# Weight sums made in the mixing stage and kept in DRAM for FFN 2 of a macaron decoder layer

## The reference

```python
def swiglu(h, w_gate, w_up, w_down):
    return (jax.nn.silu(h @ w_gate) * (h @ w_up)) @ w_down
...
x = x + 0.5 * swiglu(rmsnorm(x, ffn1_norm), ffn1_w_gate, ffn1_w_up, ffn1_w_down)
h = rmsnorm(x, mix_norm); proj = h @ w_in          # 40 blocks of weights: the mixing stage
...                                                # latent attention, HGRN2 recurrence, w_out, cross attention
x = x + 0.5 * swiglu(rmsnorm(x, ffn2_norm), ffn2_w_gate, ffn2_w_up, ffn2_w_down)
```

## Time and profile before

| | |
|---|---|
| median of 3 runs | 1886.82 us |
| the profiled execution | 1885.84 us, of which its instructions span 1884.0 us |
| TensorE: matmuls, share of the span, granted clock | 8824, 100%, 1.0 of full speed (the 2.4 GHz level) in all slices |
| TensorE's weight loads, VectorE, ScalarE, GpSimd: share of the span | 84%, 84%, 58%, 5% |
| DMA | 362.57 MB, 192 GB/s over the span, 57.4% of the 16 engines' time |
| chain of waits, by engine | TensorE 87%, VectorE 9%, issue 2%, ScalarE 1%, GpSimd 1% |

### The profile page before, as it was taken

How to read it: one execution, slowest core, us unless ns; L and a number is a source line. 1 busy time by engine, 2 the same in 40 slices (tenths; PEclk the granted TensorE clock), 3 DMA queues, 4 the chain that set the end, 5 groups by cost and what they waited for, 6 DMA issues and landing times.

```text
span 1884.0 us, 23266 instructions
## 1 busy us (share of the span) xinstructions
PE 1877.4 (100%) x8824; PEld 1575.1 (84%) x8824; DVE 1573.7 (84%) x2015; ACT 1087.4 (58%) x1473; POOL 95.4 (5%) x98
## 2 busy tenths in 40 slices
PE   9999999999999999999999999999999999999999
PEld 8888888888889888988888888888888888888987
DVE  6999999989999867755676774789999999999986
...
GB/s 337 224 196 201 193 198 193 225 201 201 181 187 213 217 224 157 167 179 179 136 156 111 206 192 139 156 181 200 201 184 195 203 205 216 204 195 184 197 192 171
DMA packets 176608, 362.57 MB, mean 192 GB/s; under 512 B 8432, under 2 KB 19696, under 8 KB 175856
## 3 DMA queue, kind: packets, MB, share of 16 engines
q1 hardware_dynamic: 176064, 360.89, 57.4%
...
...
HBM read 358.95 MB, written 2.10 MB: 192 GB/s over the span
## 4 chain that ended last, share of the span: by engine, by line
PE 87%; DVE 9%; issue 2%; ACT 1%; POOL 1%; DMA 0%; SPq 0%; DVEq 0%; ACTq 0%; POOLq 0%
PE acc L1943 16%; PE acc L1945 16%; PE acc L1944 16%; PE acc L1932 9%; PE acc L1934 8%; PE acc L1933 8%; DVE w_lo L1301 4%; PE small L1945 2%; PE small L1943 2%; PE small L1944 2%; PE small L2144 2%; PE tr L1894 1%; PE tr L1945 1%; PE tr L1943 1%; PE tr L1944 1%
## 5 line engine op out<-in xcount | busy, mean ns | idle before, releaser
L1301 DVE TENSOR_TENSOR w_lo<-w_raw,w_hi 128x1024 fp32r<-128x1024 f32 (+3 forms) x752 | 733.4, 1030 | 52.5 <-ACT w_hi L730 40.5
L730 ACT ACTIVATE w_hi<-w_raw 128x1024 fp32r<-128x1024 f32 (+4 forms) x568 | 507.9, 928 | 149.0 <-PE acc L1945 101.8
L1943 PE MATMUL acc<-w_hi,hT_hi 128*128 128x512 f32 (+1 forms) x920 | 355.0, 386 | 0.0
L1945 PE MATMUL acc<-w_lo,hT_hi 128*128 128x512 f32 (+1 forms) x920 | 353.4, 384 | 0.0
L1944 PE MATMUL acc<-w_hi,hT_lo 128*128 128x512 f32 (+1 forms) x920 | 353.1, 384 | 0.0
L1230 DVE TENSOR_TENSOR w_lo<-w_raw,w_hi 128x1024 fp32r<-128x1024 f32 (+1 forms) x184 | 218.3, 1226 | 59.6 <-ACT w_hi L730 58.2
L835 ACT ACTIVATE w_hi<-w_raw 128x1024 fp32r<-128x1024 f32 (+1 forms) x184 | 190.3, 1044 | 118.1 <-DVE w_raw L1289 72.6
L1943 PE MATMUL acc<-w_hi,actT_hi 128*128 128x512 f32 x528 | 207.1, 392 | 0.3
L1945 PE MATMUL acc<-w_lo,actT_hi 128*128 128x512 f32 x528 | 205.7, 390 | 0.0
L1944 PE MATMUL acc<-w_hi,actT_lo 128*128 128x512 f32 x528 | 205.6, 389 | 0.0
L828 ACT ACTIVATE w_hi<-w_raw 128x512 fp32r<-128x512 f32 (+3 forms) x184 | 149.4, 830 | 90.9 <-PE acc L1945 89.9
...
## 6 DMA issues: line engine op xcount, KB each, us to landing
...
w_raw<-in_ffn_w_down SPq DMA_DIRECT2D x40, 1024.0 KB, 5.3
w_raw<-in_w_in SPq DMA_DIRECT2D x36, 1024.0 KB, 5.1
...
w_raw<-in_ffn_w_up SPq DMA_DIRECT2D x26, 1024.0 KB, 5.8
```

The lines of the kernel that those rows point to most:

```text
L730: nc.scalar.activation(piece(w_hi, c % SPLIT, k0, k1, width), piece(raw, c % RAW, k0, k1, width), ACT.Copy).then_inc(hi_done, 1)
L1301: v.tensor_tensor(piece(w_lo, c % RAW, k0, k1, width), piece(raw, c % RAW, k0, k1, width), piece(w_hi, c % SPLIT, k0, k1, width).bitcast(F ...
L1943: mm(dst, lhs_hi, wh, start=first, stop=False)
L1945: return mm(dst, lhs_hi, wl, start=False, stop=last)
```

## The change

- `READY` names five up duos of FFN 2: (0,2), (0,3), (0,5), (1,0) and (1,4), the last with 384 columns. Each gets a fourth unit: its order becomes "upupuup", with plain pieces of 2, 3 and 3 k-tiles. To have a fourth set of activation sums, `H_SUMS` becomes 4 in FFN 2.
- The space for that comes from the down blocks of the first half in FFN 2: `A_SUMS` there becomes 4, their order "upupupup" with four plain pieces of 4 k-tiles. They had five units.
- Seven of the 20 units in these five duos are *ready*: units 0 and 2 of (0,2) and (0,3), unit 0 of the three others. Their weight sums are made in the mixing stage by VectorE in place (`job_first`, `job_second`, four subtractions of 128x512, in the last job 128x384), in four places of SBUF that are free at that time, from weights that SP fetches there; SP then stores them to `kept_sums` in DRAM. The seven jobs run in the steps 2, 5, 8, 20, 24, 28 and 32 of the mixing stage. SP fetches a job's weights ahead of the load of slot step + 3 and stores its sums ahead of the load of slot step + 6.
- A ready unit fetches three raw tiles and the four kept sums and has no `combine`. The other 13 units of the five duos are combined as before.

The tables and the shape of the duos:

```diff
+        H_SUMS, A_SUMS = {1: 3, 2: 4}, {1: (5, 3), 2: (4, 3)}
+        READY = {(0, 2): (0, 2), (0, 3): (0, 2), (0, 5): (0,), (1, 0): (0,), (1, 4): (0,)}
+        JOBS = [(h, b, n) for (h, b), ns in READY.items() for n in ns]
+        JOB_STEPS, JOB_PLACES = [2, 5, 8, 20, 24, 28, 32], list("ACVGGGA")
+        kept = nc.dram_tensor("kept_sums", [len(JOBS), P, 4 * NW], F32, kind="Internal").ap()
...
-                    DUOS.append(Duo(f, True, h, b, min(4, tiles - 4 * b) * P, "upupup", [0, 2, 4], [(6, 4), (10, 3), (13, 3)]))
+                    ready = READY.get((h, b), ()) if f == 2 else ()
+                    DUOS.append(Duo(f, True, h, b, min(4, tiles - 4 * b) * P,
+                                    *(("upupuup", [0, 2, 4, 6], [(8, 2), (10, 3), (13, 3)], ready) if ready else
+                                      ("upupup", [0, 2, 4], [(6, 4), (10, 3), (13, 3)]))))
                 for j in range(DB // 2):
-                    DUOS.append(Duo(f, False, h, j, NW, *(("upupupupup", [0, 2, 4, 6, 8], [(10, 3), (13, 3), (16, 3), (19, 3), (22, 2)]),
-                                                          ("upupupp", [0, 2, 4], [(6, 4), (10, 3), (13, 3), (16, 3)]))[h]))
+                    DUOS.append(Duo(f, False, h, j, NW, *(("upupupupup", [0, 2, 4, 6, 8], [(10, 3), (13, 3), (16, 3), (19, 3), (22, 2)])
+                                                          if (f, h) == (1, 0) else
+                                                          ("upupupup", [0, 2, 4, 6], [(8, 4), (12, 4), (16, 4), (20, 4)])
+                                                          if h == 0 else
+                                                          ("upupupp", [0, 2, 4], [(6, 4), (10, 3), (13, 3), (16, 3)]))))
```

SyncE, the fetch of a ready unit and the jobs' transfers:

```diff
+                    def load_ready(c, k, n):
...
+                        sp.wait_ge(slot_used, 2 * (c - RAW + 1))
...
+                        sp.dma_start(tiles[:, :, 0, 0:d.width], rows_of(wg, k, 2, cols)).then_inc(loaded[c % RAW], 16)
+                        sp.dma_start(tiles[:, 1, 1, 0:d.width], wu[(k + 1) * P:(k + 2) * P, cols]).then_inc(loaded[c % RAW], 16)
+                        sp.wait_ge(slot_used, 2 * (c + 1 - RAW + 1))
...
+                        sp.dma_start(made, kept[j].rearrange("p (k n) -> p k n", k=4)[:, :, 0:d.width]).then_inc(loaded[(c + 1) % RAW], 16)
...
+            def job_weights(j):
...
+                if earlier:
+                    sp.wait_ge(job_kept[place], 16 * earlier)
+                if place == "G" and not earlier:
+                    sp.wait_ge(ev("angles"), 1)
...
+                for u, name in enumerate(("gate", "up")):
+                    rows = rows_of(a[f"ffn2_w_{name}"][0], 2 * n, 2, slice(c0, c0 + w))
+                    sp.dma_start(tiles[:, :, u, 0:w], rows).then_inc(job_in[place], 16)
+
+            def job_store(j):
...
+                sp.wait_ge(job_made, j + 1)
...
+                sp.dma_start(dst, src).then_inc(job_kept[place], 16)
+
+            def jobs_around(m):
+
+                for j, step in enumerate(JOB_STEPS):
+                    if m == step + 6:
+                        job_store(j)
+                for j, step in enumerate(JOB_STEPS):
+                    if m == step + 3:
+                        job_weights(j)
...
                 for s in range(4):
+                    jobs_around(4 * b + s)
                     load(M + 4 * b + s, 0, rows_of(a["w_in"][0], 4 * s, 4, slice(starts[n], starts[n] + MIX_WIDTH[n])), 4, MIX_WIDTH[n])
```

VectorE, a ready unit in a duo, and the jobs in the mixing stage:

```diff
                         if kind == "u" and n:
-                            combine(d.raws[n], u0 + n, w)
-                            lo_parts(d.raws[n], RAW_PARTS, w, u0 + n)
+                            if n in d.ready:
+                                lo_parts(d.raws[n], RAW_PARTS, w)
+                            else:
+                                combine(d.raws[n], unit_number(m, n), w)
+                                lo_parts(d.raws[n], RAW_PARTS, w, unit_number(m, n))
...
-                        combine(e.raws[0], u0 + u1, e.width)
+                        if 0 not in e.ready:
+                            combine(e.raws[0], unit_number(m + 1, 0), e.width)
...
+            def job_first(j):
+
+                b = job_tiles(j)
+                dve.wait_ge(job_in[JOB_PLACES[j]], 32 * (JOB_PLACES[:j].count(JOB_PLACES[j]) + 1))
+                done(v.tensor_tensor(b[:, 0, :], b[:, 1, :], b[:, 0, :], ALU.subtract))
+                done(v.tensor_tensor(b[:, 1, :], b[:, 3, :], b[:, 1, :], ALU.subtract))
+
+            def job_second(j):
+
+                b = job_tiles(j)
+                done.wait()
+                done(v.tensor_tensor(b[:, 3, :], b[:, 3, :], b[:, 0, :], ALU.subtract))
+                done.wait()
+                v.tensor_tensor(b[:, 2, :], b[:, 2, :], b[:, 3, :], ALU.subtract).then_inc(job_made, 1)
...
             for m in range(40):
                 lo(M + m, 0, 4, MIX_WIDTH[MIX[m // 4]])
+                if m in JOB_STEPS:
+                    job_first(JOB_STEPS.index(m))
                 mixer(m)
+                if m in JOB_STEPS:
+                    job_second(JOB_STEPS.index(m))
```

More of the change, by code:

```diff
@@ L94 @@
     plains: list
+    ready: tuple = ()
     raws: list = field(default_factory=list)
@@ L249, in layer @@
         k_sq = at("k_sq", A0 + 67.5, [P, TT, ROPE])
+        job = {place: at("job_" + place, A0 + kb, [P, 4 * NW]) for place, kb in (("A", 66.5), ("C", 56), ("V", 36), ("G", 44))}
         o_mla = at("o_mla", A0 + 56, [P, TT, AH * P])
@@ L301, in layer @@
         out_done = sem("out_done")
+        job_in, job_kept = ({place: sem(f"job_{name}_{place}") for place in job} for name in ("in", "kept"))
+        job_made = sem("job_made")
         named = {}
@@ L411, in layer @@
                 fetches[r], fetches[r + 1] = 2 if duo.up else 1, 0
+            for n in duo.ready:
+                fetches[duo.raws[n] + 1] = 1
         M = slots["mix"]
@@ L428, in unit_number, with job_of @@
         def unit_number(m, n):
-            return sum(len(d.raws) for d in DUOS[:m]) + n
+            return sum(len(d.raws) - len(d.ready) for d in DUOS[:m]) + sum(i not in DUOS[m].ready for i in range(n))
+        def job_of(d, n):
+            return JOBS.index((d.half, d.block, n))
         def sums_before(f):
-            return (f - 1) * (H_SUMS + sum(A_SUMS))
+            return (f - 1) * (H_SUMS[1] + sum(A_SUMS[1]))
         def sums_number(m, n):
-            return sums_before(DUOS[m].f) + H_SUMS + sum(A_SUMS[:DUOS[m].half]) + n
+            f = DUOS[m].f
+            return sums_before(f) + H_SUMS[f] + sum(A_SUMS[f][:DUOS[m].half]) + n
         def turns_in(d):
@@ L520, in load_duos @@
                     for kind, n in d.steps():
+                        if kind == "u" and n in d.ready:
+                            load_ready(d.raws[n], d.units[n], n)
+                            continue
                         if kind == "u":
@@ L604, in _ @@
                     load(slots[2, "up", 0] + 4 * b + s, 0, rows_of(a[f"ffn2_w_{n}"][0], 4 * s, 4, slice(0, NW)), 4, NW)
+            for place in sorted(job):
+                sp.wait_ge(job_kept[place], 16 * JOB_PLACES.count(place))
             load_duos(2)
```

97 lines of the change are left out of this document (63 added, 34 removed).

## The result

The changed kernel takes **1892.76 us** (median of 7 runs, 1892.37 to 1894.46), beside 1886.79 us for the kernel before: a ratio of 1.0034, 95% interval 1.0025 to 1.0044. It is slower by 6.0 us, more than the 0.2% that a measurement can tell. I had forecast 1888.5 us and "within 0.2%". The profiled execution has a span of 1890.9 us, 6.9 more than before.

What follows compares the result with a forecast made beforehand. It took TensorE as the bound, with VectorE's splits barely ahead of it in FFN 2's up duos; -3.24 + 0.12 + 4.8 = +1.7 us gave 1887.5 profiled, 1888.5 us as median; range 1884.2 to 1893.0.

Steps and rivals of the forecast that it cites:

- within 0.2%: Whole kernel: its time would not be distinguishable from the kernel before, within 0.2% (3.8 us); chance 0.72.
- I carry no debt over: Duos behind those with late splits: VectorE regains its lead, so no loss was counted there.
- (0,2) and (0,3): "nothing": Up duos (0,2) and (0,3): unit 3's second split has a lead of 0.8 us, so no loss; 41.76 us each.
- The stalls inside (0,5), (1,0) and (1,4): Late VectorE splits in these up duos cost 1.9, 0.3 and 2.6 us, together +4.8 us.
- Rival 1: Adjacent units in up duos: VectorE is about 1.2 us further ahead, avoiding most stalls; 1884.5 us, chance 0.18.
- rival 3: Up duos: ScalarE's splits are late too after a late combine, doubling the 4.8 us loss; 1893.3 us, chance 0.12.
- the forecast's own spread: Whole kernel: the main forecast, given chance 0.55, spans 1886.5 to 1890.5 us.
- the range over all cases: Whole kernel: forecast and rivals together span 1884.2 to 1893.0 us.
- The down duos: FFN 2's first-half down duos: six more matmuls, but 1.24 us of waiting goes; together 126.10 us, +0.12 us.
- The mixing stage: Seven jobs add 18 us of VectorE work, covered by 100 us of its idle time: 0, with +3 as bound.
- The tight place: Mixing stage, job 0: its subtractions delay slot 3's splits but stay covered, with 0.5 us to spare.
- The 0.11 us surcharge of a wait: TensorE at a late split: it loses the lateness plus 0.11 us, as the next matmul comes late.

Runs made afterwards that it cites:

- Run 2: The change with (1,4)'s kept sums used for unit 0 of (0,4) instead, (0,4) and (1,4) keeping three units: 1887.91 us.
- run 5: The change with ScalarE making w_hi of the last second-side piece before its two Silus in FFN 2, no work added or removed: 1888.46 us.
- runs 6 and 7: The change with unit 2 ready instead of unit 0 in (0,5) and (1,4): 1890.38 us; the same plus ScalarE's Silus behind w_hi in FFN 2: 1884.45 us.
- under 8: Several versions; meant here: the kernel before with ScalarE's Silus behind w_hi of the last second-side piece, in both FFNs: 1885.19 us.

## Why the prediction was wrong

- **The step that failed** is the sentence "Behind the late blocks one combine less (before a duo whose unit 0 is ready) or slack in the down blocks takes VectorE back to its lead, so I carry no debt over". Only (0,2) has a ready unit 0 behind it. Behind (0,3), (0,5), (1,0) and (1,4) the next unit 0 is combined, and the second side had lost two tiles, 2.72 us of cover. Only behind (0,5) was there the slack that I counted on. Measured: 3.9 us in (0,4), (1,1), (1,2) and the down duo, where I put nothing; in (0,4) and the down duo at unit 0, in (1,1) and (1,2) at unit 2. Run 2 shows it for (0,4) by the missing combine, run 5 for all four by the missing round trip. The figures were at hand: TensorE's cover by matmuls, and the idle time of VectorE in the kernel before at the end of each duo. I followed VectorE through each duo from its first matmul and stopped at unit 3.
- **(0,2) and (0,3): "nothing"** was wrong as well. I had worked out unit 3 only. Unit 1 stands behind a piece that shrank from four tiles to two, and is late by 0.26 and 0.45 us.
- **The stalls inside (0,5), (1,0) and (1,4)** were right: 1.92, 0.36 and 2.61 us measured (the duo's length less what its matmuls and turns take), 1.9, 0.3 and 2.6 forecast. So was their cause, by runs 6 and 7. Rival 1, that a hidden lead holds, is out.
- **The range and rival 3.** 1892.76 us lies above the forecast's own spread (1886.5 to 1890.5) and just inside the range over all cases (to 1893.0). Rival 3 gave 1893.3, but that it comes near is luck: its sign, waits of VectorE for ScalarE inside units 2 and 3, is absent. In (0,5) and (1,4) the profile shows one wait of VectorE for ScalarE each, 1.76 and 1.46 us, behind the last unit. What was right in it is that ScalarE comes first, in another place.
- **The down duos:** +0.11, forecast +0.12. Of the 1.24 us of waits that went, 0.66 (0.33 in each duo, at 1498.26 and 1560.49 in the kernel before) was not of the kind in the earlier trace rows but TensorE waiting for `take_parts`, as under 8; the last piece of four tiles took that away as well.
- **The mixing stage** costs nothing, as forecast; the profile shows no wait of TensorE in it. The tight place was job 0. VectorE there, in the changed kernel:

```profile
701.20 0.68 DVE L1766 TENSOR_TENSOR job_A<-job_A 128x512 f32<-128x512 f32 x1
701.80 0.68 DVE L1767 TENSOR_TENSOR job_A<-job_A 128x512 f32<-128x512 f32 x1
...
708.49 0.68 DVE L1773 TENSOR_TENSOR job_A<-job_A 128x512 f32<-128x512 f32 x1
709.20 0.69 DVE L1775 TENSOR_TENSOR job_A<-job_A 128x512 f32<-128x512 f32 x1
709.81 2.35 DVE L1311 TENSOR_TENSOR w_lo<-w_raw,w_hi 128x1024 fp32r<-128x1024 f32 x2
```

  and TensorE's first matmul of slot 3:

```profile
711.76 0.39 PE L2043 MATMUL acc<-w_hi,hT_hi 128*128 128x512 f32 x1
```

  The first split is done at 709.81 + 1.13 + 0.08 = 711.02, a lead of 0.7 us; I had 0.5. A job's four ops take 0.68 us each, 2.7 in all, for the 2.6 that I took from combine. The Trainium skill ("VectorE: DVE Perf Modes", the section on the TRN2 errata) gives (N + 151) / 0.96 for an fp32 tensor_tensor, 691 ns at 512 elements and, worked out from it as an estimate, 1224 at 1024; this trace agrees, with 0.68 to 0.69 and 1.22 us.
- **The 0.11 us surcharge of a wait** holds: the matmul behind the one that waited comes 0.30 to 0.34 us later and not 0.23 (1371.49 to 1371.83). The Trainium skill ("TensorE: Matmul & The Clock Gate", Architectural detail) would have the next weight load pulled ahead during the wait; at none of the waits that I read is the distance 0.23. At the wait of 1370.36 the profile shows that load only after it, 0.10 us behind the matmul that had waited:

```profile
1370.46 0.19 PEld L2055 LDWEIGHTS tr<-w_hi,hS_lo 128*128 128x128 f32 x1
```

In one sum, by duos: -3.24 (matmuls) + 0.11 (down pair) + 4.89 (stalls forecast) + 0.71 (unit 1) + 3.90 (debts) = +6.37 us. The start of the second half's last down duo is 6.90 us later than before, 0.53 of it already at the first duo of FFN 2; 0.47 of that stands at the first duo of FFN 1 (51.97 us for 51.50), whose code is the same.
